# Row projections of a two-layer and NSA/PEER model: the third and fourth quarters of the normed X transposed between units

## The reference

```python
# layers 1 and 2 (layer 0 and 1 in the kernel)
h = _rms_norm(x, g_pre)                       # x: [1, 256, 2048]
proj = jnp.einsum('bsd,de->bse', h, w_in)     # w_in: [2048, 7232]
...
return x + _rms_norm(y, g_post)               # y: attention output @ w_out
# the block behind them
h = rmsnorm(x, g_norm_mix[l]) * (1.0 + scale1) + shift1
... = split_cols(h @ w_in[l], IN_SIZES)
```

## Time and profile before

| | us |
|---|---|
| median of 3 runs | 2998.16 |
| lowest and highest of the 3 | 2998.08, 3005.84 |
| profiled execution, its own time | 3002.68 |
| profiled execution, span | 3001.0 |
| PE busy | 2928.6 (98% of the span) |
| DVE busy | 2141.1 (71%) |
| ACT busy | 1303.6 (43%) |
| TensorE clock, mean granted share | 0.99 |

### The profile page before, as it was taken

The page is one execution under the profiler, slowest core; times in us unless marked ns, Lnnn a source line. Parts: engine busy times, 40 slices in busy tenths (PEclk is TensorE's granted clock), DMA queues, the critical chain, the costliest instruction groups (busy, mean ns, idle before and its releaser), DMA issues.

```text
span 3001.0 us, 43372 instructions
## 1 busy us (share of the span) xinstructions
PE 2928.6 (98%) x16000; PEld 2479.1 (83%) x16000; DVE 2141.1 (71%) x2847; ACT 1303.6 (43%) x1655; POOL 312.1 (10%) x345
## 2 busy tenths in 40 slices
PE   7999999999999999999999999999999999999997
PEld 6888788888788888887888888888888888877886
DVE  6687777686775767677479688547884478888745
ACT  5343444443553433454345444444444444444443
POOL 1001020011021101010067300000000000000001
PEclk9999999999999999899999999999999999999999
DMA  8857477776567877246545554555455554445553
GB/s 319 291 216 277 160 260 258 266 246 247 181 235 247 290 280 257 95 167 225 182 147 177 181 181 173 186 189 194 171 179 182 196 185 180 182 170 181 189 191 138
DMA packets 99608, 620.53 MB, mean 207 GB/s; under 512 B 11056, under 2 KB 11184, under 8 KB 37040
## 3 DMA queue, kind: packets, MB, share of 16 engines
q1 hardware_dynamic: 70560, 509.88, 47.4%
q0 software_dynamic: 28944, 109.26, 10.1%
HBM read 616.99 MB, written 2.10 MB: 206 GB/s over the span
## 4 chain that ended last, share of the span: by engine, by line
PE 86%; DVE 7%; DMA 2%; issue 2%; ACT 2%; POOL 1%; DVEq 0%; POOLq 0%; SPq 0%; ACTq 0%
PE ps L533 25%; PE ps L497 17%; PE ps L906 17%; PE ps L535 13%; PE ps L958 5%; DMA aring<-in_ada 2%; DVE wl L1734 1%; PE ps L870 1%; PE ps L694 1%; ACT BIG L1022 1%; ACT wh L1022 1%; DVE aring L1750 1%; PE ps L748 1%; DVE BIG L2195 1%; PE ps L618 0%
## 5 line engine op out<-in xcount | busy, mean ns | idle before, releaser
L1022 ACT ACTIVATE wh<-ring 128x2048 fp32r<-128x2048 f32 (+1 forms) x499 | 896.5, 1802 | 1349.7 <-PE ps L535 711.7
L1734 DVE TENSOR_TENSOR wl<-ring,wh 128x2048 fp32r<-128x2048 f32 (+1 forms) x434 | 988.4, 2277 | 629.0 <-ACT wh L1022 362.5
L533 PE MATMUL ps<-hhl,wh 128*128 128x512 f32 x3712 | 1320.1, 400 | 12.5 <-DVE wl L1734 3.5
L535 PE MATMUL ps<-hhl,wl 128*128 128x256 f32 x3712 | 1040.2, 280 | 0.0
L533 PEld LDWEIGHTS ps<-hhl,wh 128*128 128x128 f32 x3712 | 699.3, 188 | 179.1 <-issue 10.6
L535 PEld LDWEIGHTS ps<-hhl,wl 128*128 128x128 f32 x3712 | 703.1, 189 | 0.1
L497 PE MATMUL ps<-wh,hhl 128*128 128x512 f32 (+1 forms) x1728 | 529.7, 387 | 5.9 <-issue 4.5
L497 PEld LDWEIGHTS ps<-wh,hhl 128*128 128x128 f32 x1728 | 323.3, 189 | 75.8 <-DVE wl L1734 7.9
L497 PE MATMUL ps<-wl,hhl 128*128 128x512 f32 (+1 forms) x864 | 333.1, 385 | 0.0
L1750 DVE SCALAR_TENSOR_TENSOR aring<-aring,BIG 128x1024 f32<-128x1024 f32 x192 | 233.3, 1220 | 29.8 <-DMA aring<-in_ada 28.1
L906 PE MATMUL ps<-wh,stage_h 128*128 128x512 f32 x744 | 199.0, 389 | 2.0 <-issue 2.0
(11 more groups left out here) (284 smaller groups left out, 2489.0 us busy)
## 6 DMA issues: line engine op xcount, KB each, us to landing
ring<-in_stream SPq DMA_DIRECT2D x480, 1024.0 KB, 4.8
aring<-in_ada POOLq DMA_DIRECT2D x192, 512.0 KB, 5.1
BIG<-in_nbr_bias POOLq DMA_DIRECT2D x2, 1024.0 KB, 6.2
BIG<-in_g_post POOLq DMA_DIRECT2D x2, 1024.0 KB, 5.1
out<-X SPq DMA_DIRECT2D x4, 512.0 KB, 3.8
BIG<-in_decays POOLq DMA_DIRECT2D x2, 768.0 KB, 5.1
X<-in_x SPq DMA_DIRECT2D x1, 1024.0 KB, 7.0
X<-in_x SPq DMA_DIRECT2D x2, 512.0 KB, 9.0
```

Of the source, the lines that this page charges most:

```text
L533: mm(ps[:, 4 + c, :], wh[:, c % 2, w], hhl[:, k, :, :].rearrange("p a b -> p (a b)"), start=(k == 0), stop=False, skip_group_check=True)
L535: last = mm(ps[:, 4 + c, 0:SEQ], wl[:, c % 2, w], hh[:, k, :], start=False, stop=(k == KD - 1), skip_group_check=True)
L1022: return nc.scalar.activation(o, i, func, **kw)
L1734: return tt(blocks(wl[:, c % 2, :], cols), blocks(ring[:, c, :], cols), blocks(wh[:, c % 2, :].bitcast(F32), cols), ALU.subtract)
```

## The change

Quarter 2 is no longer transposed ahead of the first unit in the two layers. In all three first groups, quarter 2 is now transposed between units 0 and 1, and quarter 3 between units 1 and 2. On DVE, in the two layers, `normed` (and in layer 1 `x_block`) of quarter 2 moves from ahead of bank 0 to behind bank 1; quarter 3 keeps its place. In the block behind, only PE's order changes. `keep_awake` at the end of each layer does 32 matmuls, not 40. ACT's order is as it was.

```diff
--- before.py
+++ after.py
@@ -503,9 +503,8 @@
                 if not begun:
                     pe.wait_ge(tm_free, n + 1)
                 for s in range(R):
-                    if s == 1:
-                        for norm, part in rest:
-                            transposed(norm, part)
+                    if 0 < s <= len(rest):
+                        transposed(*rest[s - 1])
                     if s or not begun:
                         if use is not None:
                             operand_part(use, s)
@@ -561,10 +560,10 @@
             with pe.Fori(0, LAYERS) as l:
-                for part in range(3):
+                for part in range(2):
                     transposed(l, part)
                 for i in range(TM_G - 2):
-                    rows_group(l * LAYER_G + i, l * TM_N + i, i % 2, layer=None if i else l, rest=() if i else ((l, 3),))
+                    rows_group(l * LAYER_G + i, l * TM_N + i, i % 2, layer=None if i else l, rest=() if i else ((l, 2), (l, 3)))
@@ -696,7 +695,7 @@
-                keep_awake(40, 7)
+                keep_awake(32, 7)
@@ -1802,13 +1801,17 @@
                 dve.wait_ge(prs_done, l + 1)
-                for block in range(3):
+                def begin(block):
+
                     if l:
-                        if block == 2:
+                        if block > 1:
                             x_block(l - 1, block)
                         next_block(l - 1, block)
                     else:
                         normed(block)
+
+                begin(0)
+                begin(1)
                 for b in range(8):
@@ -1816,13 +1819,11 @@
                     ins.then_inc(nl_done, 1)
-                    if b == 3:
+                    if b == 1:
+                        begin(2)
+                    elif b == 3:
                         next_low(l * LAYER_G, 0)
-                        if l:
-                            x_block(l - 1, 3)
-                            next_block(l - 1, 3)
-                        else:
-                            normed(3)
+                        begin(3)
                     elif b == 5:
                         next_low(l * LAYER_G, 1)
```

## The result

The changed kernel takes 3009.73 us (median of 5 runs, 3009.23 to 3016.65); the kernel before, timed again beside it, 3001.38 (5 runs, 2998.08 to 3005.84). The medians lie 8.4 us apart. The ratio is 1.0034, with a 95% interval of 1.0022 to 1.0047: slower by 10 us, between 7 and 14. The forecast was 3008.4, 10.2 above the median of before. A single run says little here: the runs of one kernel lie 7 to 20 us apart.

The account below looks back on a forecast made before the run. PE, busy for 98% of the span, was taken to bound the kernel, its stalls paid in full. Terms 4.1 + 1.2 + 0.9 + 1.0 + 2.6 + 0.4 = 10.2 us on 2998.16 gave 3008.4, range 3002 to 3014.

Parts of the forecast that it names:

- The main step: Layer 0: quarter 3's later transposes delay its chain to `wl`, so PE idles 3.8 us and unit 3 starts 4.1 later.
- the first transposes were granted 1.2 GHz: Layer 0 start: the first 24 transposes, 0.20 us apiece, ran at half speed; the clock rose just before 21.
- The rows' price of the table load: ACT, layer 0: load and `Silu` together take 3.12 us; an added drain would make the term +5.5, not +4.1.
- The clock in layer 0: Behind the 3.8 us stall ahead of unit 3, PE runs partly at half speed: +1.2, bounds 0 and 1.7.
- The clock in layer 1: Lower clock behind unit 3's wait and at the start of layer 1: +1.0, with bounds of 0 and 2 x 1.7.
- Layer 1 and the block: Layer 1's unit 3 starts 0.9 later; in the block behind, unit 3 starts 2.6 later, plus 0.4 for the clock.
- The start of layer 1: With shorter `keep_awake` and quarter 2 moved on DVE, unit 0 of layer 1 starts at 451.1, 1.4 earlier.
- (c): All three places: quarter 3's chain is in time, only starts' gains remain: -2, 2996; 0.13 including cases towards (b).
- (e): Layer 0, unit 0: transposes don't raise the clock, so it stays at 1.2 GHz at first: +1.7, 3010; chance 0.03.
- (b): Waits come, but the clock hardly drops, or no longer drops in the block's unit 0: 3004 to 3007; chance 0.25.
- (d): The clock drops at all the places, at the starts too: 13.5, up to 15, 3011 to 3013; chance 0.12.
- (a): The forecast as summed over all three places: +9 to +12.5, 3007 to 3011; chance 0.47.

Follow-up runs that it names:

- ka40: The changed kernel with `keep_awake` back at 40 matmuls; ratio 1.0038 to the kernel before, median 3014.28 us.
- tm2: The changed kernel with quarters 2 and 3 both transposed behind unit 0 in the block behind, as before the change; ratio 1.0014 to the kernel before.
- lowfirst: The changed kernel with `low_part(2)` ahead of `shifted(3)` on DVE in the block behind; one run took 3009.96 us.
- fill: The changed kernel with 15 unread float32 matmuls ahead of unit 3 of the first group in both layers; one run took 3006.51 us.
- early: The changed kernel with layer 0's `Silu` ahead of bank 4, unit 3's `wl` ahead of both modulations, the block's transposes as before; ratio 1.0043, median 3014.03 us.
- between: As early, but with `wl` of unit 3 between the two modulations; ratio 1.0019 to the kernel before, median 3005.65 us.
- ka32_fill: The kernel before with `keep_awake` of 32 matmuls and 10 unread float32 matmuls ahead of unit 0 in the block behind; ratio 1.0.
- after_again: The changed kernel, unaltered, traced a second time; it took 3016.09 us.
- silu: The changed kernel with `Silu` on ACT moved from behind bank 7 to ahead of bank 4 in layer 0; ratio 1.0028, median 3009.06 us.
- before_again: The kernel before, unaltered, traced a second time; the three places sum to 104.7 us, the rest of the span is 2893.0 us.

## Why the prediction was right

**The main step held.** "Quarter 3's chain moves with its transposes" gave +4.1 in layer 0 and measured +4.65. The transposes came at 32.89, not 32.3: unit 0 took 6.21 us (26.53 - 20.32), not 5.7, since the low clock lasted further into it than the 0.2 us allowed for. The chain from ACT's copy to `wl` was as computed, 40.66 - 33.53 = 7.13 for 7.10. One reading behind the step needs a word: it says that the first transposes were granted 1.2 GHz. The profile's clock view gives 1.00 for that stretch, so half speed is read there from the durations alone (0.20 us a transpose for 0.10, and first matmuls of 0.79 and 0.63 as behind the wait, where the view gives 0.50). The rows' price of the table load held too: `Silu` starts 1.30 behind the load (36.41 - 35.11), right at the end of its 1.28. The Trainium skill (ScalarE: Activation LUTs, "What ACT_TABLE_LOAD costs") adds a drain of about 1.38 us to each switch. This trace shows none.

**The clock in layer 0 was mis-sized**: 1.2 forecast, bounds 0 to 1.7, and 2.8 measured. The step took a fall of 1.7 behind a wait of 2.69 as the upper bound for a longer wait. Nothing in the rows bounded it so. All five traces with that wait (both of the changed kernel, ka40, tm2, lowfirst) have 5.8 to 6.1 us at half speed, so at this place it isn't chance. Run fill shows that the idling causes it. But the length of a wait does not set the length of the stretch: behind 4.35 us, in early, it lasted 3.5 us, and behind 2.69 us in the block 1.7 us were lost in one trace of before and nothing in the other.

**The clock in layer 1** was forecast at +1.0 and cost nothing, in either trace of the changed kernel. In early, between and ka32_fill the same place did run at half speed, and in between it cost 2.2 us (unit 0 took 7.74 us). So a term of 0 to some 2 us belongs there which varies between executions.

**Layer 1 and the block** came out at +1.1 for +0.9 and at +3.4 for +3.0. The start of layer 1 was right (4.49 us from `normed` to unit 0, for 4.4): the prediction took both limits into account, the end of `keep_awake` and the quarter on DVE, and the runs show that each hides the gain of removing the other.

**Luck.** The terms add up to 12.0 in the first pair of traces and to 11.4 in the second. That the ratio gives 10.2 to the tenth is chance, and so is a part of the 12.0: the errors of the two clock terms, +1.6 and -1.0, partly cancel.

**The rivals.** (c), not slower, fell at the point named for it: `wl` of unit 3 was 3.6 us late. (e) fell: unit 0 of layer 0 took 26.53 - 20.32 = 6.21 us, 0.75 more than 5.46 and not 1.7 more. (b) fell in its first part, since the clock did drop behind the long wait, in five of five traces. Its second part did happen: in after_again the block's unit 0 ran at full speed (5.56 us), which was also named as a sign of a wrong forecast. It was none. Unit 3 of the block started at +29.0 all the same, since PE then waited for `wl` and `hhl` instead. (d) fell, as no clock was lost at the start of layer 1. Of the five runs, three lie within (a)'s 3007 to 3011, one within (d)'s 3011 to 3013, and one above both.

**What stays open.** The interval, 7 to 14 us, can't tell 10.2 from 12.0. What chooses between the two paces of a loop, and what sets how long a half-speed stretch lasts, is not shown by any run.

## What to carry to other kernels

Moving a step later on the bound engine moves everything queued behind its consumers; follow the in-order queues to the last instruction that the bound engine needs, and not only to the operand that was moved. The gain at the start was 0.7 us in layer 0, of which 0.1 was left one unit later, and 1.3 in layer 1; it was paid for with one unit of cover. Where two things limit a start, as `keep_awake` and quarter 2 did in layer 1, taking away one shows nothing. When a wait is cured by reordering, look at which load the delayed instruction frees a buffer for: early turned a wait of 1.55 us (in silu) into one of 4.35. And where runs of one kernel spread over 10 us, compare times from an anchor inside the trace, such as the first `normed` of a stage: terms of 0.2 us could be read there.

## What was not expected of the hardware

- Behind 3.6 us of idling TensorE ran at half speed for about 6 us, longer than the idling itself (five of five traces with that wait; 42.80 to 48.74 in ka40, 43.04 to 49.15 in tm2). Behind 4.35 us, in early, it was 3.5 us (50.00 to 53.50).
- The same loop ran at 5.55 or 5.65 us a unit with the full clock granted, in two executions of one program; no row shows what chooses.
- TensorE's way around its hardware loop took 1.45 us from the last `keep_awake` matmul to the next pass's first transpose (before and ka40; 1.75 in before_again). Behind the second pass, where no way back is taken, it was 0.22, and there TensorE waited for `normed`. With 32 matmuls `normed` came last in layer 1 too, after 2.08 us of idling.
